# The gated layer of a two-block network with its weights as stationary operand

## The reference

```python
h2 = rms_norm_2(x, ffn_norm_g)
return x + (jax.nn.silu(h2 @ w_ffn_gate) * (h2 @ w_ffn_up)) @ w_ffn_down
```

## Time and profile before

| | |
|---|---|
| median of three runs | 2034.02 us |
| the profiled execution | 2034.01 us |
| its span | 2032.1 us |
| mean granted clock of TensorE | 0.982 |
| TensorE busy | 1971.4 us, 97% |
| VectorE busy | 1285.1 us, 63% |
| ScalarE busy | 922.1 us, 45% |
| split L411 on VectorE | 648 times, mean 1237 ns |
| w_hi L402 on ScalarE | 648 times, mean 1051 ns |
| matmuls L444, L451 from h_hi and h_lo | 3 x 2332, mean 398, 388, 389 ns |

### The profile page before, as it was taken

One profiled execution on the slowest core, in us unless ns is written; L12 is line 12 of the kernel. 1 busy time (PEld: TensorE's weight loads), 2 busy tenths in 40 slices (PEclk: granted clock), 3 DMA queues, 4 the chain that ended last, 5 costly groups with the idle time before them and its releaser, 6 DMA issues.

```text
span 2032.1 us, 23567 instructions
## 1 busy us (share of the span) xinstructions
PE 1971.4 (97%) x9253; PEld 1577.1 (78%) x9253; DVE 1285.1 (63%) x1634; ACT 922.1 (45%) x1214; POOL 385.7 (19%) x588
## 2 busy tenths in 40 slices
PE   5699999999999999999999999999999999999999
PEld 0088887777878888777888888888888888888887
DVE  1578789797666689788865664654454444454443
ACT  1166534555544544444554444544444444443332
POOL 0000007999999930000000000000000000000000
PEclk6799999999999999999999999999999999999999
DMA  9967677555566775454446555555556655655554
GB/s 392 412 230 244 213 235 220 176 187 165 162 219 212 206 214 186 146 176 154 150 156 197 187 187 187 185 187 187 188 192 194 193 187 186 195 179 197 195 187 165
DMA packets 193971, 407.93 MB, mean 201 GB/s; under 512 B 8843, under 2 KB 15044, under 8 KB 189124
## 3 DMA queue, kind: packets, MB, share of 16 engines
q1 hardware_dynamic: 178208, 376.07, 55.8%
q10 hardware_dynamic: 13892, 23.88, 3.5%
q0 software_dynamic: 1760, 6.49, 1.6%
HBM read 404.31 MB, written 2.10 MB: 200 GB/s over the span
## 4 chain that ended last, share of the span: by engine, by line
PE 87%; DVE 7%; DMA 4%; ACT 1%; issue 1%; ACTq 0%; DVEq 0%
PE ps L444 53%; PE ps L451 26%; PE pm L537 4%; DMA raw<-in_ada_w 3%; DVE raw_lo L411 2%; PE pm L549 1%; DVE sc_i L1288 1%; PE ps L537 1%; DVE xtmp L1371 1%; PE pm L914 0%; DMA raw<-in_w_in 0%; ACT w_hi L402 0%; PE pm L599 0%; DVE gate L1197 0%; DVE proj L1303 0%
## 5 line engine op out<-in xcount | busy, mean ns | idle before, releaser
L411 DVE TENSOR_TENSOR raw_lo<-raw,w_hi 128x1024 fp32r<-128x1024 f32 (+1 forms) x648 | 799.6, 1237 | 553.4 <-ACT w_hi L402 544.1
L402 ACT ACTIVATE w_hi<-raw 128x1024 fp32r<-128x1024 f32 (+1 forms) x648 | 680.4, 1051 | 785.7 <-PE ps L451 758.2
L444 PE MATMUL ps<-w_hi,h_hi 128*128 128x512 f32 (+1 forms) x2332 | 925.7, 398 | 5.4 <-DVE h_lo L997 4.5
L444 PE MATMUL ps<-w_hi,h_lo 128*128 128x512 f32 (+1 forms) x2332 | 904.5, 388 | 0.0
L451 PE MATMUL ps<-raw_lo,h_hi 128*128 128x512 f32 (+1 forms) x2332 | 621.8, 389 | 5.8 <-DVE raw_lo L411 5.8
L444 PEld LDWEIGHTS ps<-w_hi,h_hi 128*128 128x128 f32 x2332 | 438.9, 188 | 102.0 <-issue 6.8
L451 PEld LDWEIGHTS ps<-raw_lo,h_hi 128*128 128x128 f32 x2332 | 436.2, 188 | 99.4 <-DVE raw_lo L411 9.5
L444 PEld LDWEIGHTS ps<-w_hi,h_lo 128*128 128x128 f32 x2332 | 439.5, 188 | 89.8 <-issue 4.6
L2342 POOL TENSOR_TENSOR proj<-proj 128x128 f32<-128x128 f32 x264 | 189.4, 722 | 12.9
L2342 POOL TENSOR_TENSOR proj<-proj,w1T 128x128 f32<-128x128 f32 x165 | 97.7, 600 | 11.9 <-DMA proj<-in_z 4.7
L444 PE MATMUL ps<-w_hi,hid_hi 128*128 128x512 f32 x256 | 99.9, 390 | 0.0
(11 more groups left out here) (332 smaller groups left out, 1107.8 us busy)
## 6 DMA issues: line engine op xcount, KB each, us to landing
raw<-in_w_in SPq DMA_DIRECT2D x136, 1024.0 KB, 5.3
raw<-in_w_ffn_gate SPq DMA_DIRECT2D x44, 1024.0 KB, 5.2
raw<-in_w_ffn_up SPq DMA_DIRECT2D x44, 1024.0 KB, 5.2
raw<-in_w_ffn_down SPq DMA_DIRECT2D x44, 1024.0 KB, 5.1
raw<-in_ada_w SPq DMA_DIRECT2D x32, 1024.0 KB, 9.1
raw<-in_w_out SPq DMA_DIRECT2D x32, 1024.0 KB, 5.1
proj<-in_ada_w ACTq DMA_DIRECT2D x16, 1024.0 KB, 6.5
raw<-in_w_br_hyena SPq DMA_DIRECT2D x8, 1024.0 KB, 5.1
```

What stands on the lines that cost most here:

```text
L402: nc.scalar.activation(w_hi[:, p % HRING, :, 0:gm.width(j)], raw[:, k % RING, e:e + HT, 0:gm.width(j)], ACT.Copy).then_inc(hi_done, 1)
L411: nc.vector.tensor_tensor(raw_lo[:, k % RING, e:e + HT, 0:gm.width(j)], raw[:, k % RING, e:e + HT, 0:gm.width(j)], w_hi[:, p % HRING, :, 0 ...
L444: nc.tensor.matmul(ps[pair][:, t, 0:gm.width(j)], l[:, tok], hi[:, i, 0:gm.width(j)], start=(k == 0 and l is x_hi), stop=False)
```

## The change

In `g_f` the roles of the operands are exchanged. A 128x128 piece of the weights is stationary and all 256 tokens of a k-tile of `h_hi` or `h_lo` are moving. The output comes out turned: 128 features on the partitions, 256 tokens along the bank, so that a pair of banks holds four pieces of 128 features. Each part has 2 k-tiles x 4 pieces x 3 = 24 matmuls of 256 columns. In the w_hi half two matmuls in a row (h_hi, h_lo) have the same stationary operand.

The activation is then already in the form that the down projection wants: `turn_act` goes, with its semaphores and its use of `pm`, and `act_highs` and `act_lows` read `act_t` in one operation of 1024 columns. But 1/rms is now a factor per column, not per partition. A row of 256 factors on all partitions, `row_scales`, is made once: VectorE multiplies `ident` by the factors, TensorE multiplies that by `ones` (two f32 matmuls between the first two groups), VectorE copies the result into `gate`, which is free by then. ScalarE can't apply it within Silu, so VectorE multiplies the gate group by it first (`scale_gate`), ScalarE takes Silu in place, and VectorE multiplies by the up group and once more by `row_scales` (`activate`). All of these are single operations of 128x1024. `g_d` and everything ahead of `g_f` are as they were.

```diff
+                if turned:
+                    acc = ps[pair][:].rearrange("p t (c n) -> p (t c) n", c=2)
+                    pe.wait_ge(hi_done, p + 1)
+                    for i in range(HT):
+                        k = HT * n + i
+                        for c in range(CK):
+                            for q, x in enumerate(stat(k, j)):
+                                nc.tensor.matmul(acc[:, c], hi[:, i, c * P:c * P + P], x, start=(k == 0 and c % 2 == 0 and q == 0),
+                                                 stop=False, skip_group_check=True)
+                    pe.wait_ge(lo_done, p + 1)
+                    for i in range(HT):
+                        k = HT * n + i
+                        for c in range(CK):
+                            mm = nc.tensor.matmul(acc[:, c], lo[:, i, c * P:c * P + P], stat(k, j)[0], start=False, stop=(k == kt - 1),
+                                                  skip_group_check=True)
+                    mm.then_inc(mm_done, 1)
...
-            def turn_act(g):
-
-                pe.wait_ge(sig("act_ready"), g + 1)
-                for u in range(2):
-                    pe.wait_ge(sig("act_used"), g * 2 + (u + 1))
-                    for k in (2 * u, 2 * u + 1):
-                        for t in range(TT):
-                            o = ((k % 2) * TT + t) * P
-                            i = nc.tensor.transpose(act_bank(g, u)[:, o:o + P], act_t[:, act_slot(g), t, k * P:k * P + P], ident[:])
-                    i.then_inc(sig("act_turned"), 1)
...
             for g in range(n_ff):
-                multiply_group(pe, g_f, 2 * g, halves, made("h3") if g == 0 else None, beside if g == 0 else None)
-                if 1 <= g <= main:
-                    turn_act(g - 1)
-                multiply_group(pe, g_f, 2 * g + 1, halves)
...
+                multiply_group(pe, g_f, 2 * g, halves, made("h3") if g == 0 else None, beside if g == 0 else None, turned=True)
+                if g == 0:
+                    pe.wait_ge(sig("scale_diag"), TT)
+                    b = bank(pe, "scale", "v")
+                    for t in range(TT):
+                        m = mm(b[:, t * P:t * P + P], ones[:], scale_diag[:, t * P:t * P + P])
+                    m.then_inc(filled, 1)
+                multiply_group(pe, g_f, 2 * g + 1, halves, turned=True)
...
             def act_lows(g):
-                for u in range(2):
-                    dve.wait_ge(sig("act_hi"), g * 2 + (u + 1))
-                    v.tensor_tensor(hidden(h_lo, hid_lo, g, u), act_bank(g, u)[:, :], hidden(h_hi, hid_hi, g, u).bitcast(F32),
-                                    ALU.subtract).then_inc(sig("act_used"), 1)
+                dve.wait_ge(sig("act_hi"), g + 1)
+                v.tensor_tensor(hidden(h_lo, hid_lo, g), act_t[:, act_slot(g)], hidden(h_hi, hid_hi, g).bitcast(F32),
+                                ALU.subtract).then_inc(sig("hidden_lo"), 1)
+
+            def scale_gate(g):
+                multiplied(dve, g_f, 2 * g)
+                if g >= 2:
+                    dve.wait_ge(sig("hidden_lo"), min(g, main + 1) - 1)
+                v.tensor_tensor(act_t[:, act_slot(g)], turned_pair(g_f, 2 * g), scales, ALU.mult).then_inc(evac[pair_of(g_f, 2 * g)], 1)
 
             def activate(g):
-                pair = multiplied(dve, g_f, 2 * g + 1)
-                evacuated(dve, g_f, 2 * g)
+                multiplied(dve, g_f, 2 * g + 1)
+                dve.wait_ge(sig("silu_made"), g + 1)
                 act = act_t[:, act_slot(g)]
-                for t in range(TT):
-                    i = v.scalar_tensor_tensor(act[:, t], pair[:, t], rr[:, 1, t:t + 1], act[:, t], ALU.mult, ALU.mult)
...
+                v.tensor_tensor(act, turned_pair(g_f, 2 * g + 1), act, ALU.mult).then_inc(evac[pair_of(g_f, 2 * g + 1)], 1)
                 evacuated(dve, g_f, 2 * g + 1)
-                dve.sem_inc(sig("act_ready"), 1)
+                v.tensor_tensor(act, act, scales, ALU.mult).then_inc(sig("act_ready"), 1)
+                dve.wait_ge(sig("act_ready"), g + 1)
+
+            dve.wait_ge(sig("h3_scale"), 1)
+            for t in range(TT):
+                v.tensor_scalar(scale_diag[:, t * P:t * P + P], ident[:], rr[:, 1, t:t + 1], None, ALU.mult).then_inc(sig("scale_diag"), 1)
...
                 for n in range(g_f.parts):
                     low(dve, g_f, 2 * g + 1, n)
+                    if n == HRING - 2:
+                        if g == 0:
+                            link(v.tensor_copy(row_scales, content(dve, "scale", "v")[:, 0:SEQ]))
+                            dve.sem_inc(used["v"], 1)
+                        scale_gate(g)
...
             def act_highs(g):
-                for u in range(2):
-                    act.wait_ge(sig("act_turned"), g * 2 + (u + 1))
-                    s.activation(hidden(h_hi, hid_hi, g, u), act_bank(g, u)[:, :], ACT.Copy).then_inc(sig("act_hi"), 1)
+                act.wait_ge(sig("act_ready"), g + 1)
+                if g >= main:
+                    act.wait_ge(mm_done, g_f.end())
+                s.activation(hidden(h_hi, hid_hi, g), act_t[:, act_slot(g)], ACT.Copy).then_inc(sig("act_hi"), 1)
...
-                        for t in range(TT):
-                            i = s.activation(act_t[:, act_slot(g), t], pair[:, t], ACT.Silu, scale=rr[:, 1, t:t + 1])
...
+                        evacuated(act, g_f, 2 * g)
+                        s.activation(act_t[:, act_slot(g)], act_t[:, act_slot(g)], ACT.Silu).then_inc(sig("silu_made"), 1)
```

More of the change, by code:

```diff
@@ L308, in build @@
         hid_lo = sb("hid_lo", [P, FT_MAIN, SEQ], F32R, st)
-        act_t = sb("act_t", [P, 3, TT, GW], F32, st)
+        act_t = sb("act_t", [P, 3, GW // P, SEQ], F32, st)
         st.close()
@@ L412, in low, with multiply_group @@
               .then_inc(lo_done, 1)
-        def multiply_group(pe, gm, j, stat, before=None, beside=None, rows=False):
+        def multiply_group(pe, gm, j, stat, before=None, beside=None, rows=False, turned=False):
             pair = pair_of(gm, j)
@@ L436, in multiply_group @@
                     break
+                if turned:
[14 more added lines that the diff above has]
+                    mm.then_inc(mm_done, 1)
+                    if beside is not None:
+                        beside.step(p)
+                    continue
                 pe.wait_ge(hi_done, p + 1)
@@ L510, in hidden_halves, with hidden @@
             return h_hi[:, k - FT_MAIN], h_lo[:, k - FT_MAIN]
-        def hidden(below, main_room, g, u):
+        def hidden(below, main_room, g):
             room, k = (main_room, 4 * g) if 4 * g < FT_MAIN else (below, 4 * g - FT_MAIN)
-            return room[:, k + 2 * u:k + 2 * u + 2].rearrange("p k n -> p (k n)")
+            return room[:, k:k + 4]
         def mix_rows_of(u):
@@ L526, in build, with turned_pair @@
         REST_AT = (0, 2, 4)
-        def act_bank(g, u):
-            return pm[2 * (g % 2) + u]
+        row_scales, scale_diag = gate[:, 0:SEQ], gate[:, SEQ:2 * SEQ]
+        def turned_pair(gm, j):
+            return ps[pair_of(gm, j)][:].rearrange("p t (c n) -> p (t c) n", c=2)
         def act_slot(g):
@@ L904, in _, with hidden_made @@
             multiply(pe, g_o2, halves, made("mg"), beside)
-            def turn_act(g):
-                pe.wait_ge(sig("act_ready"), g + 1)
-                for u in range(2):
-                    pe.wait_ge(sig("act_used"), g * 2 + (u + 1))
-                    for k in (2 * u, 2 * u + 1):
-                        for t in range(TT):
-                            o = ((k % 2) * TT + t) * P
-                            i = nc.tensor.transpose(act_bank(g, u)[:, o:o + P], act_t[:, act_slot(g), t, k * P:k * P + P], ident[:])
-                    i.then_inc(sig("act_turned"), 1)
-            pe.sem_inc(sig("act_used"), 4)
             main = FT_MAIN // 4
             for g in range(n_ff):
-                multiply_group(pe, g_f, 2 * g, halves, made("h3") if g == 0 else None, beside if g == 0 else None)
-                if 1 <= g <= main:
-                    turn_act(g - 1)
-                multiply_group(pe, g_f, 2 * g + 1, halves)
-            def turn_rest(n):
-                if n in REST_AT:
-                    turn_act(main + REST_AT.index(n))
+                multiply_group(pe, g_f, 2 * g, halves, made("h3") if g == 0 else None, beside if g == 0 else None, turned=True)
[6 more added lines that the diff above has]
+                multiply_group(pe, g_f, 2 * g + 1, halves, turned=True)
+            def hidden_made(n):
                 if n == FT_MAIN // HT:
-                    pe.wait_ge(sig("act_used"), 2 * n_ff + 4)
-            pe.wait_ge(sig("act_used"), 2 * main + 4)
+                    pe.wait_ge(sig("hidden_lo"), n_ff)
+            pe.wait_ge(sig("hidden_lo"), main)
             for j in range(g_d.groups):
-                multiply_group(pe, g_d, j, hidden_halves, turn_rest if j == 0 else None, rows=j == g_d.groups - 1)
```

(12 more changed lines are left out.)

7 lines of the change are left out of this document (1 added, 6 removed).

## The result

| | before | after |
|---|---|---|
| median, same chip | 2034.11 us (4 runs) | 2056.16 us (4 runs, 2055.15 to 2056.69) |
| ratio to before, 95% interval | | 1.011 (1.0092 to 1.0127) |
| profiled execution, span | 2034.01, 2032.1 us | 2055.73, 2053.9 us |
| mean granted clock | 0.982 | 0.982 |

A forecast was written before the change was run, and what follows sets the result against it. TensorE was taken to bound the gated layer. Matmuls +28.1, transposes -8.9, change of layer +1.2 and `ones` matmuls +0.45 sum to +20.9 us: 2055 us, slower by 1.0%, range 2045 to 2073.

The forecast's parts named there:

- The bound: Gated layer, 1299 to 1786 us: TensorE busy all 487 us at clock 1.00; other engines' time worth nothing within their slack.
- The price of a matmul: Gate and up projections: 0.120 us per 256-column matmul against 0.2267 for 512; 2112 replaced by 4224, +28.1 us.
- the formula of the Trainium skill: Warm matmul spacing of N/2.4 + 2.5 ns: 109.2 ns for 256 columns, which would make the gated layer shorter.
- the record of a load: A stationary operand's load record lasts 0.188 us, longer than a 256-column matmul; taken as latency, with a pace of 0.110 us.
- The rival of load behind matmul: Gated layer: the 0.0133 us follows a load of 0.110, so 0.1235 us per matmul; 2070 us, chance 0.12.
- that of the load's pace alone: Gated layer: the 0.0133 us disappears and only the load's 0.110 us remains per matmul; faster, 2013 us, chance 0.07.
- The reading of c_sig: First-stage modulation: one c_sig column serves four matmuls in a row with 256 loads for 256 matmuls; so one load per matmul.
- The transposes: TensorE's 88 transposes of act_t go: 0.89 us a block, ten of eleven blocks on the path, -8.9 us.
- The sum: Whole kernel: 28.1 - 8.9 + 1.2 + 0.45 = +20.9 us on 2034.0, giving 2055 us; chance 0.74.
- The change of layer: Gated layer to down projection: two dependent VectorE operations before the first split, 2.71 us for 1.54; +1.2 us, bounds 0 to 3.
- the eleventh block: Transposes at the start of the down projection only filled part of TensorE's wait for VectorE; removing them gives nothing.
- Hidden items: Waits for the `ones` matmuls' inputs and the added VectorE and ScalarE work fit in slack, costing nothing; the matmuls themselves +0.45 us.

The follow-up runs named there:

- The halved kernel: Kernel before with each gated-layer matmul of 512 columns made two of 256, weights still moving, transposes and old activation kept: 2061.54 us, ratio 1.0137.
- the run with transposes: Changed kernel with eleven blocks of eight 128x128 transposes of the identity matrix put back where they stood: 2064.11 us, ratio 1.0149.
- Ten waits of 7.0 us: Changed kernel with twelve more dependent VectorE operations of 128x1024 behind every scale_gate from the second pair on: 2142.35 us in one run.

## Why the prediction was right

1. **The bound.** TensorE at clock 1.00 and waited for by all: it holds after the change too (508.50 of 508.50 us busy), and four extra VectorE operations a pair change nothing.
2. **The price of a matmul.** 0.120 us by extrapolation from 512 and 296 columns, 0.120 in the trace. This term made the forecast: it decided against the formula of the Trainium skill ("TensorE: Matmul & The Clock Gate", section "Back-to-back issue gap"), by which the layer would have got shorter, and against the record of a load, 0.188 us, at which 4224 of them would have taken 794 us. The halved kernel measures it alone: 28.2 us against 28.1. The rival of load behind matmul (0.1235) and that of the load's pace alone (0.110) are out at 256 columns; the second one's floor is real but begins under some 230 columns. The reading of c_sig (256 loads for 256 matmuls) counts records, two for each of 128 f32 instructions; its conclusion holds, 4224 loads in the layer. Some of the exactness is luck: the straight line through 512 and 296 columns was taken to go on below them, and it does at 256 columns, but 248+264 and 264+248 stand 7 and 3 ns under it. For pieces of 248 and 264 in this order the same working would have come out 14 us too high (2112 x 6.7 ns, an estimate from those means).
3. **The transposes.** 8.9 us forecast; putting them back costs 8.0 to 8.4 by the medians and 8.7 in the traces. They stand 0.109 us apart, twice the 0.053 of their columns. The prediction put that down to the load; two passes of f32, which the f32 records of 256 and 512 columns show, would take as long, and no run tells the two apart. The sum doesn't hang on it.
4. **The change of layer.** The two operations took 1808.69 to 1811.21, 2.52 us, where the sum had 2.71; so everything was 1.0 us later than before rather than 1.2, and putting the activation behind two splits gives the 2.3 us back. What the sum lacked is the clock behind that wait: 1.6 us in one of the six profiles that have it, nothing in the others. The forecast's reason, that the eleventh block fills a wait, shows in the run with transposes.
5. **Hidden items.** The f32 matmuls for `row_scales` came without a wait of TensorE. VectorE and ScalarE stayed in their slack.
6. **The sum.** The span grew by 21.9 us in the unrounded trace, against 20.9. Of that the layer has 21.3 (21.4 forecast) and the rest of the span -0.7 (-0.6), together 20.6. Another 1.3 us lies ahead of the layer, where nothing was changed: it began at 1300.3 in place of 1299.05. Over all fourteen traces it begins anywhere from 1297.1 to 1300.3 us. From its start to the end of the span the other profile of the changed kernel has 22.2 us more than before, with the 1.6 us of low clock in it. The forecast had no term for either, and that its median is met within 1.2 us is no more exact than that.

## What to carry to other kernels

A matmul has a price apart from its columns, and it depends on the number format: here about 13 ns in float32r and 3 in bf16. Read it from starts at two widths before halving the width of a long stream; a saving beside it (88 transposes, 8 to 9 us) must be set against that price times the whole count (4224 matmuls, 28 us). And when an activation is split in more steps in a row, look at the place where the next layer's first input is queued behind the last of them: there the steps show at full length, and in one of six profiles the clock added 1.6 us to them. Moving that one behind the next layer's first splits cost nothing in either kernel here.

## What the runs showed of the hardware that was not expected

- The addition of 13 ns comes with float32r, by its loads or by its columns: bf16 matmuls of 256 columns stand 110 ns apart and f32 passes of 512 at 429 ns for two.
- Full loads of 128 columns pace float32r matmuls at 108 to 112 ns; in bf16 128 columns go at 57 ns with full loads, so that the pace depends on the format too.
- For some uneven cuts of 512 columns a pair is cheaper than the 240 ns of 256+256, and the order counts: 233 for 248+264 and 237 for 264+248, 236 for 272+240 but 240 for 240+272. With 272+240 over the whole layer it is 8.2 us in the trace. Not explained.
- Ten waits of 7.0 us cost more than their 70 us: the layer's granted clock went from 1.00 to 0.94 with them, and the run was 86.6 us longer. TensorE's 2.0 us wait at the change of layer left its clock at 1.00 in five profiles; in the sixth it fell to 0.57 over the 4 us from 1812, which cost 1.6 us.
